# A trunk of attention and convolution on one core: four query tiles to a value product, and a quarter of the softmax combination on GpSimd

## The chip, the cores and the metric

One core of a Trainium2 chip (trn2). The metric is device time in microseconds of one launch; 2425.22 us is the median of three runs of the kernel before.

## What is computed

A float32 trunk of two layers over 1024 tokens of width 1024: differential attention with a convolutional feed-forward network behind it, then a gated short convolution with a second such network, then a norm. Only attention is touched by the change. For each of 8 heads:

```python
s = jnp.einsum('bqhcd,bkhcd->bhcqk', q_blk, k)          # c = 0, 1: two score maps
p = jax.nn.softmax(s, axis=-1)
a = p[:, :, 0] - lam * p[:, :, 1]
o = jnp.einsum('bhqk,bkhe->bqhe', a, v)                 # v is 128 wide
o = rms_norm(o, subln_g) * (1.0 - lambda_init)
```

## The kernel before

The program is written out by hand for each engine: every engine has its own list of instructions, which it works off in order, and semaphores tie them together. Matrix products keep float32 accuracy by splitting an operand into a rounded part (fp32r) and the rest, and summing three products. Activations lie with features on the 128 partitions.

The stages in order are: norm and projections to q, k, v, written to memory (till about 303 us); attention (303 to 645 us); output projection; feed-forward; convolution layer; second feed-forward. The output projection of the first two tiles (`dense_ahead`) already stands in the tail of attention.

**Attention** runs through 64 steps, 8 heads x 8 tiles of 128 queries. Each engine has a function `step(h, ii)` and `run_steps` calls them (steps of the middle heads in a hardware loop over pairs of heads). `i` counts the steps. PSUM has four slots of 1024 columns: slots 0 and 1 for the two score maps of a tile, one buffer each, slot 2 for transposes, slot 3 for the value product and, in its other half, the sum of squares.

What happens to a tile `i`, and in which step, is:

- TensorE, step i: `scores`, 4 products of 128x512 for each map (L656, L657). The first map waits for the first exponential of the tile before, the second map for the second one (`e_done`).
- VectorE, step i: `minimum` (L1281) over the 1024 columns of each map, the first and the second.
- ScalarE, step i: exponential of the first map (L962) into P0, with its row sum, and of the second map (L974) into P1. Between the two stands the rounding of the transposes of tile i-2 (L969).
- Step i+1: VectorE takes the reciprocal of a row sum (L1291) between its two minima; GpSimd makes the row's coefficient out of it in two small steps (L1549, L1552); VectorE combines the softmaxes, P1 = P1 * coef + P0 (L1300, called the combination below), 1024 columns. It is left unnormalised by the first row sum; that cancels in the norm behind it, if epsilon is scaled with the square of the row sum. GpSimd puts this square on a diagonal times epsilon (`dg`, L1558).
- Step i+2: TensorE transposes the combination, 8 blocks (L664); ScalarE rounds it (L969) into `Ah`; VectorE makes the rest (L1306) into `Al`.
- Once per pair of tiles: the value product (L679), 24 products of 256 columns, 12 in each of two steps; ScalarE copies it with a scale (L990) and squares it (L992); TensorE sums the squares and the epsilon diagonals over the partitions (L687, L690); ScalarE makes the factor (L983, L985); GpSimd multiplies (L1571); ScalarE rounds the result to Yh (L996) and GpSimd makes the rest Yl (L1565).

The order within a step is fixed: on TensorE scores, transposes, sum of squares, values; on ScalarE first exponential, rounding, second exponential, then the work of the pairs; on VectorE first minimum, reciprocal, second minimum, combination, rest; on GpSimd coefficient, square, diagonal, Yl, multiplication. SyncE loads K, Q and V of the next head, each once its buffer is free.

Of the kernel before, what the change touches and what calls it, by code (L numbers as in the profile page):

```python
# [80 lines left out]
def build(nc, x_in, positions, weights, ups, params_in, consts_in, lams_in, out):  # L81
    ctx = ExitStack()
    with ctx:
# [20 lines left out]
        coef = sb("coef", [P, 4])  # L104
        epsb = sb("epsb", [P, 1])
# [26 lines left out]
        W_more = at("W_more", [P, 2, 1024], AR + 70 * K, F32R)  # L132
        Wraw_more = at("Wraw_more", [P, 1024], AR + 70 * K + 4 * K)
# [52 lines left out]
        def q_set(h, parity):  # L186
            return 2 if is_first(h) else parity
# [42 lines left out]
        inv_done, co_done, a_done, t_done = sem("inverse_done"), sem("coef_done"), sem("a_done"), sem("t_done")  # L230
        ah_made, al_made = sem("ah_made"), sem("al_made")
        s0sq_done, dg_done = sem("s0sq_done"), sem("dg_done")
        pv_half = sem("pv_half")
# [132 lines left out]
        def lagged(q, first, tail):  # L366
            return (not first or q >= 0) and (not tail or q < QT)

        def on(q, first, tail):

            return q % 2 == 0 and lagged(q, first, tail)

        def run_steps(eng, step, last):
            for ii in range(QT):
                step(0, ii, first=True, parity=0)
            with eng.Fori(0, HEADS // 2 - 1) as pair:
                for a in range(2):
                    for ii in range(QT):
                        step(pair * 2 + (1 + a), ii, parity=1 - a)
            for ii in range(QT):  # L380
                step(HEADS - 1, ii, parity=1)
            for ii in range(QT, last + 1):
                step(HEADS - 1, ii, tail=True, parity=1)
# [22 lines left out]
        def _(sp):  # L406
# [84 lines left out]
            def load_head(h, parity, first=False):  # L491
# [8 lines left out]
                if not first:  # L500
                    sp.wait_ge(pv_done, 4 * (h - 1))
# [105 lines left out]
        def _(pe):  # L607
# [1120 lines left out]
```

## Time and profile before

| | |
|---|---|
| Median of 3 runs | 2425.22 us (2424.23 to 2425.43) |
| The profiled execution | 2422.12 us, span 2420.3 us |
| TensorE busy | 2350.3 us, 97% |
| VectorE busy | 1357.0 us, 56% |
| ScalarE busy | 949.7 us, 39% |
| GpSimd busy | 1050.0 us, 43% |
| Mean granted TensorE clock | 0.993 |

The shares are means over all stages. Rows name lines of the kernel before (L1300) and tiles as out<-in. PE is TensorE, PEld its weight loads, DVE VectorE, ACT ScalarE, POOL GpSimd. A matrix product's length in the trace has its fill in it; the distance from one start to the next is what it costs in a train of them.

### The profile page before, as it was taken

To read this page: it belongs to the slowest core of one execution; us is meant where nothing else is said; L and a number is where in the kernel's file an instruction comes from. 1 tells how busy PE (TensorE), PEld (TensorE's weight loads), DVE (VectorE), ACT (ScalarE), POOL (GpSimd) and SP (SyncE) were. 2 spreads that over 40 slices of the span, in tenths; PEclk is the share of its full clock that TensorE was granted. 3 is DMA by queue.
4 is the path that set the end of the run, shared out by engine and by line. 5 is a ranking of instruction groups with operands and counts; after the bars stand their busy time and mean duration, and the time that the engine had idled before them with its cause. 6 is when DMAs were issued, how large, how long until landed. Compare 5 with 4: busy or idle time off the path is not lost.

```text
span 2420.3 us, 28034 instructions
## 1 busy us (share of the span) xinstructions
PE 2350.3 (97%) x10948; PEld 1947.1 (80%) x10948; DVE 1357.0 (56%) x1240; ACT 949.7 (39%) x1149; POOL 1050.0 (43%) x725
## 2 busy tenths in 40 slices
PE   8899989999999999999999999999999999999997
PEld 6688778888877888888888888888878888888886
DVE  7566799999475555556422233344655555564223
ACT  5111278888444444444311321113454444442112
POOL 1112134444367677775122422213687666742221
PEclk9899999999999999999999999999999999999998
DMA  3453373432222222222522111112222222234222
GB/s 129 165 173 122 131 214 101 120 98 76 86 83 84 87 79 79 87 88 99 197 90 81 56 44 49 47 52 87 96 70 93 81 87 79 79 131 174 90 79 93
DMA packets 73799, 239.45 MB, mean 99 GB/s; under 512 B 8160, under 2 KB 8544, under 8 KB 73696
## 3 DMA queue, kind: packets, MB, share of 16 engines
q1 hardware_dynamic: 73696, 238.01, 29.9%
q8 instruction: 72, 1.18, 0.2%
q14 instruction: 31, 0.25, 0.0%
HBM read 177.16 MB, written 60.82 MB: 98 GB/s over the span
## 4 chain that ended last, share of the span: by engine, by line
PE 76%; issue 13%; ACT 4%; DVE 3%; POOL 3%; DMA 0%; POOLq 0%; DVEq 0%; ACTq 0%
PE PS L282 35%; PE PS L766 11%; PE PS L767 11%; PE PS L768 11%; PE PS L679 2%; DVE nb L1281 2%; POOL Wst L267 2%; PE PS L656 1%; PE PS L657 1%; PE PS L664 1%; ACT X L962 1%; ACT X L974 1%; ACT sq L974 1%; POOL X L1621 1%; PE PS L690 1%
## 5 line engine op out<-in xcount | busy, mean ns | idle before, releaser
L267 POOL TENSOR_TENSOR Wst<-Wraw,Wst 128x1024 fp32r<-128x1024 f32 (+1 forms) x111 | 263.0, 2371 | 877.5 <-ACT Wst L261 877.5
L766 PE MATMUL PS<-XB,U 128*128 128x512 f32 x1208 | 471.1, 390 | 6.9 <-POOL U L1615 6.8
L768 PE MATMUL PS<-XB,U 128*128 128x512 f32 x1224 | 476.7, 389 | 0.0
L282 PE MATMUL PS<-H,Wst 128*128 128x512 f32 x2070 | 470.1, 389 | 0.6 <-issue 0.3
L767 PE MATMUL PS<-XB,U 128*128 128x512 f32 x1208 | 470.4, 389 | 0.0
L282 PEld LDWEIGHTS PS<-H,Wst 128*128 128x128 f32 x2070 | 388.4, 188 | 81.9 <-issue 1.3
L282 PE MATMUL PS<-XGh,Wst 128*128 128x512 f32 x1536 | 420.3, 394 | 25.5 <-POOL Wst L267 13.0
L261 ACT ACTIVATE Wst<-Wraw 128x1024 fp32r<-128x1024 f32 (+1 forms) x111 | 113.9, 1028 | 652.3 <-DMA Wraw<-weights 652.2
L282 PEld LDWEIGHTS PS<-XGh,Wst 128*128 128x128 f32 x1536 | 290.1, 190 | 89.2 <-issue 24.6
L766 PEld LDWEIGHTS PS<-XB,U 128*128 128x128 f32 x1208 | 227.1, 188 | 55.9 <-POOL U L1615 7.6
L768 PEld LDWEIGHTS PS<-XB,U 128*128 128x128 f32 x1224 | 230.0, 188 | 48.0
L767 PEld LDWEIGHTS PS<-XB,U 128*128 128x128 f32 x1208 | 227.2, 188 | 46.8
L282 PE MATMUL PS<-XGl,Wst 128*128 128x512 f32 x768 | 239.0, 393 | 0.0
L1615 POOL TENSOR_TENSOR U<-U1f,U 128x2048 fp32r<-128x2048 f32 x44 | 203.8, 4631 | 6.0
L1077 ACT ACTIVATE PS<-rawg,par 128x1024 f32<-128x1024 f32 x44 | 53.2, 1210 | 385.9 <-DVE rawg L1400 385.9
L282 PEld LDWEIGHTS PS<-XGl,Wst 128*128 128x128 f32 x768 | 145.9, 190 | 30.8
L1281 DVE TENSOR_REDUCE nb<-PS 128x1 f32<-128x1024 f32 x128 | 154.1, 1210 | 15.9 <-PE PS L657 15.9
L1423 DVE TENSOR_TENSOR H<-Hf,H 128x1024 fp32r<-128x1024 f32 x44 | 71.2, 1619 | 142.0 <-ACT H L1086 141.8
L1615 POOL TENSOR_TENSOR U<-U2f,U 128x1536 fp32r<-128x1536 f32 x42 | 149.3, 3554 | 0.0
L1579 POOL TENSOR_TENSOR U1f<-U2f 128x512 f32<-128x512 f32 x44 | 57.9, 1316 | 208.0 <-DMA U2f<-ups 208.0
L282 PE MATMUL PS<-Yh,Wst 128*128 128x512 f32 x480 | 130.3, 390 | 2.7 <-POOL Wst L267 2.7
L1411 DVE SCALAR_TENSOR_TENSOR PS<-rawg,par,PS 128x1024 f32<-128x1024 f32 x88 | 113.4, 1289 | 28.6 <-ACT PS L1077 27.1
(191 smaller groups left out, 3311.2 us busy)
## 6 DMA issues: line engine op xcount, KB each, us to landing
Wraw<-weights SPq DMA_DIRECT2D x79, 512.0 KB, 3.5
U1f<-ups SPq DMA_DIRECT2D x44, 512.0 KB, 4.6
U2f<-ups SPq DMA_DIRECT2D x44, 512.0 KB, 3.8
h_scratch<-Tv SPq DMA_DIRECT2D x44, 512.0 KB, 5.4
Hf<-h_scratch SPq DMA_DIRECT2D x44, 512.0 KB, 4.7
Wraw<-weights SPq DMA_DIRECT2D x32, 448.0 KB, 3.2
x_scratch<-X SPq DMA_DIRECT2D x16, 512.0 KB, 3.1
X<-x_scratch SPq DMA_DIRECT2D x16, 512.0 KB, 7.1
```

The costliest lines, as they stand in the source:

```text
L261: act.activation(w[:, 0, 0:cols], raw[:, 0:cols], ACT.Copy).then_inc(w_hi, 1)
L267: pool.tensor_tensor(w[:, 1, 0:cols], raw[:, 0:cols], w[:, 0, 0:cols].bitcast(F32), ALU.subtract).then_inc(w_lo, 1)
L282: ins = pe.matmul(ps[:, h * HALF:(h + 1) * HALF], w, m[:, h * HALF:(h + 1) * HALF], start=begin, stop=last and w is wl)
L766: pe.matmul(ps, wh, bh, start=begin, stop=False, skip_group_check=True)
L767: pe.matmul(ps, wh, bl, start=False, stop=False, skip_group_check=True)
L768: ins = pe.matmul(ps, wl, bh, start=False, stop=kp == KP - 1, skip_group_check=True)
L1077: act.activation(conv_ps(kind), src[:, 1:S + 1], ACT.Identity, bias=ffn_col(l, p, kind, 3), scale=ffn_col(l, p, kind, 1)).then_inc(f["mid" ...
L1281: dve.tensor_reduce(nb[:, b:b + 1], slot(c), axis=AX_X, op=ALU.min).then_inc(nb_done, 1)
L1411: dve.scalar_tensor_tensor(out=T, in0=raw[:, off:off + S], scalar=ffn_col(l, p, kind, c), in1=T, op0=ALU.mult, op1=ALU.add).then_inc(f["ta ...
L1423: dve.tensor_tensor(Hs[t][:, 1, :], Hf[t][:, :], Hs[t][:, 0, :].bitcast(F32), ALU.subtract).then_inc(f["hl"], 1)
L1579: pool.tensor_tensor(U1f[s][:, 1, O_S1, :], U2f[s][:, 1, 1, :], U2f[s][:, 1, 2, :], ALU.add).then_inc(f["sums"], 1)
L1615: pool.tensor_tensor(u[s][:, 1, :, :], uf[s][:, 1, :, :], u[s][:, 0, :, :].bitcast(F32), ALU.subtract).then_inc(f["lo"], 1)
```

## The change

Four tiles of queries now go to one value product. `At` holds the rounded parts and the rests of two groups of four tiles; each group has one half of its own and one that both share. The value product is 24 products of 512 columns, of which 9, 12 and 3 stand in the steps ii-6, ii-7 and ii-8 of the group's first tile, the last 3 ahead of the transposes. ScalarE's and GpSimd's work on a result comes once in four steps and 512 columns wide, its order and its steps are new. The epsilon diagonals are added to the squares on GpSimd, and TensorE sums both with one instruction.

VectorE combines columns 0 to 767; GpSimd multiplies and then adds the last 256, each with an instruction of its own. Transposes and the next first exponential wait for both parts. There is no loop left: all 64 steps are written out. The third tile of the output projection (`W_more`) lies 2 KB further on. SyncE's waits on `pv_done` count groups of four. (`lagged` and `on` are as before, but with `q % 4`.)

```diff
-        Ah = [XGl[:, 2 * b:2 * b + 2, :].rearrange("p a (t n) -> p (a t) n", n=2 * P) for b in range(2)]
-        Al = [XGl[:, 4 + 2 * b:6 + 2 * b, :].rearrange("p a (t n) -> p (a t) n", n=2 * P) for b in range(2)]
-        osq, osb, z, ot = (sq[:, 0, t * 2 * P:(t + 1) * 2 * P] for t in range(4))
-        ot3 = sq[:, 0:1, 6 * P:8 * P]
-        dg = cu[:, 0:QT * P]
+            return 2 if h == 0 else parity
+        At = at("At", [P, 17, 2 * S], AR + 32 * K, F32R)
+        A_HI, A_LO = ((1, 16), (2, 16)), ((0, 4), (3, 4))
+        on_q = at("on_q", [P, 4, HALF], AR + 148 * K)
+        osq, osb, z, ot = (on_q[:, t, :] for t in range(4))
+        dg = at("dg", [P, HALF], ER + 16 * K)
+        def a_tile(where, q):
+            block = where[q // 4][q // 2 % 2]
+            return At[:, block, :].rearrange("p (t n) -> p t n", n=2 * P)[:, :, q % 2 * P:(q % 2 + 1) * P]
+        def a_group(where, g, t):
+            b0, b1 = where[g]
+            return At[:, b0:b1 + 1:b1 - b0, t * 2 * P:(t + 1) * 2 * P]
...
                 pe.wait_ge(a_done, i + 1)
+                pe.wait_ge(a_rest, i + 1)
                 wait(pe, al_made, i)
...
-            def values(h, u, quarter, part, parity):
-                b = quarter % 2
+            def values(h, u, g, part, parity):
                 if part == 0:
-                    pe.wait_ge(al_made, 2 * u + 2)
-                    wait(pe, o_sq, u)
-                if quarter == 0 and part == 0:
+                    pe.wait_ge(al_made, 4 * u + 4)
+                    wait(pe, o_copied, u)
+                if g == 0 and part == 0:
                     pe.wait_ge(v_in, 32 * (h + 1))
-                for t in range(4 * part, 4 * part + 4):
+                for t in (range(0, 3), range(3, 7), range(7, 8))[part]:
                     c = slice(t * P, (t + 1) * P)
-                    for w, m in ((0, Ah[b]), (0, Al[b]), (1, Ah[b])):
-                        first, last = t == 0 and w == 0 and m is Ah[b], t == KT - 1 and w == 1
-                        ins = pe.matmul(slot(3)[:, 0:2 * P], VV[parity][w][:, c], m[:, t, :], start=first, stop=last)
-                ins.then_inc((pv_half, pv_done)[part], 1)
-            def subln_sum(u, quarter):
-                pe.wait_ge(o_sq, u + 1)
-                pe.wait_ge(dg_done, 2 * u + 2)
+                    for w, m in ((0, A_HI), (0, A_LO), (1, A_HI)):
+                        first, last = t == 0 and w == 0 and m is A_HI, t == KT - 1 and w == 1
+                        ins = pe.matmul(slot(3)[:, 0:HALF], VV[parity][w][:, c], a_group(m, g, t),
+                                        start=first, stop=last)
+                if part == 2:
+                    ins.then_inc(pv_done, 1)
+            def subln_sum(u):
+                pe.wait_ge(sqd_done, u + 1)
                 wait(pe, ln_done, u)
-                pe.matmul(slot(3)[:, HALF:HALF + 2 * P], ones[:, :], osq, start=True, stop=False)
-                for t in range(2):
-                    b = 2 * quarter + t
-                    ins = pe.matmul(slot(3)[:, HALF + t * P:HALF + (t + 1) * P], ones[:, :],
-                                    dg[:, b * P:(b + 1) * P], start=False, stop=t == 1)
-                ins.then_inc(ss_done, 1)
+                pe.matmul(slot(3)[:, HALF:S], ones[:, :], osq, start=True, stop=True).then_inc(ss_done, 1)
...
+            def step(h, ii, tail=False):
+                i, parity = h * QT + ii, h % 2
...
+                if on(h, ii - 8, tail):
+                    values_of(8, 2)
+                if lagged(h, ii - 2, tail):
                     transposes(i - 2, (ii - 2) % QT)
-                if on(ii - 6, first, tail):
-                    subln_sum(h * 4 + (ii - 6) // 2, (ii - 6) // 2 % 4)
-                if on(ii - 4, first, tail):
-                    values(h, h * 4 + (ii - 4) // 2, (ii - 4) // 2 % 4, 0, parity if ii >= 4 else 1 - parity)
-                if on(ii - 5, first, tail):
-                    values(h, h * 4 + (ii - 5) // 2, (ii - 5) // 2 % 4, 1, parity if ii >= 5 else 1 - parity)
-                if tail:
-                    dense_ahead(*((0, (0, 1)), (0, (2, 3)), (0, (4, 5, 6)), (1, (0, 1, 2)), (1, (3, 4, 5, 6)))[ii - QT])
+                if on(h, ii - 10, tail):
+                    subln_sum(h * 2 + (ii - 10) // 4)
+                if on(h, ii - 6, tail):
+                    values_of(6, 0)
+                if on(h, ii - 7, tail):
+                    values_of(7, 1)
+                if tail and ii - QT in ahead:
+                    dense_ahead(*ahead[ii - QT])
...
+            def step(h, ii, tail=False):
                 i = h * QT + ii
                 if not tail:
                     act.wait_ge(nb_done, 2 * i + 1)
                     wait(act, a_done, i - 1)
+                    wait(act, a_rest, i - 1)
...
-                if lagged(ii - 2, first, tail):
+                if lagged(h, ii - 2, tail):
                     q = (ii - 2) % QT
                     act.wait_ge(t_done, i - 1)
-                    if q % 2 == 0:
-                        wait(act, pv_done, h * 4 + (ii - 2) // 2 - 1)
-                    act.activation(Ah[q // 2 % 2][:, :, q % 2 * P:(q % 2 + 1) * P],
-                                   slot(2).rearrange("p (t n) -> p t n", n=P), ACT.Copy).then_inc(ah_made, 1)
+                    if q % 4 == 0:
+                        wait(act, pv_done, h * 2 + (ii - 2) // 4 - 1)
+                    if q % 4 == 2:
+                        wait(act, pv_done, h * 2 + (ii - 2) // 4)
+                    act.activation(a_tile(A_HI, q), slot(2).rearrange("p (t n) -> p t n", n=P), ACT.Copy
+                                   ).then_inc(ah_made, 1)
...
+                if on(h, ii - 10, tail):
...
                     act.wait_ge(ss_done, u + 1)
...
+                    wait(act, o_scaled, u)
+                    act.activation(z, slot(3)[:, HALF:S], ACT.Ln, scale=1.0 / VD).then_inc(ln_done, 1)
...
+                if on(h, ii - 8, tail):
+                    u = h * 2 + (ii - 8) // 4
                     act.wait_ge(pv_done, u + 1)
+                    wait(act, ss_done, u)
+                    act.activation(osq, slot(3)[:, 0:HALF], ACT.Square).then_inc(o_sq, 1)
                     wait(act, o_scaled, u)
-                    act.activation(osb, slot(3)[:, 0:2 * P], ACT.Copy, scale=lam[:, 5:6]).then_inc(o_copied, 1)
-                    wait(act, ss_done, u)
-                    act.activation(osq, slot(3)[:, 0:2 * P], ACT.Square).then_inc(o_sq, 1)
-                if on(ii - 8, first, tail):
-                    u, uq = h * 4 + (ii - 8) // 2, (ii - 8) // 2
+                    act.activation(osb, slot(3)[:, 0:HALF], ACT.Copy, scale=lam[:, 5:6]).then_inc(o_copied, 1)
...
+                if on(h, ii - 12, tail):
+                    u = h * 2 + (ii - 12) // 4
                     act.wait_ge(o_scaled, u + 1)
-                    act.activation(Yh[:, bass.ds(h + uq // 4, 1), uq % 4 * 2 * P:(uq % 4 + 1) * 2 * P], ot3, ACT.Copy
+                    act.activation(Yh[:, u // 2, u % 2 * HALF:(u % 2 + 1) * HALF], ot, ACT.Copy
                                    ).then_inc(yh_made, 1)
...
-                    dve.scalar_tensor_tensor(out=P1[q % 4], in0=P1[q % 4], scalar=coef[:, 3:4],
-                                             in1=P0[q % 2], op0=ALU.mult, op1=ALU.add).then_inc(a_done, 1)
-                if lagged(ii - 2, first, tail):
+                    dve.scalar_tensor_tensor(out=P1[q % 4][:, main_cols], in0=P1[q % 4][:, main_cols],
+                                             scalar=coef[:, 3:4], in1=P0[q % 2][:, main_cols], op0=ALU.mult,
+                                             op1=ALU.add).then_inc(a_done, 1)
...
+                    dve.tensor_tensor(a_tile(A_LO, q), slot(2).rearrange("p (t n) -> p t n", n=P),
+                                      a_tile(A_HI, q).bitcast(F32), ALU.subtract).then_inc(al_made, 1)
...
+                    wait(pool, a_rest, i - 1)
                     pool.tensor_tensor(coef[:, 3:4], coef[:, 1:2], rsum[:, 0, q:q + 1], ALU.mult).then_inc(co_done, 1)
-                    wait(pool, dg_done, i - 1)
-                    pool.tensor_tensor(coef[:, 2:3], rsum[:, 0, q:q + 1], rsum[:, 0, q:q + 1], ALU.mult
+                    pool.wait_ge(co_done, 2 * i)
+                    rest = P1[q % 4][:, rest_cols]
+                    pool.tensor_tensor(rest, rest, coef[:, 3:4].to_broadcast([P, S // 4]), ALU.mult
+                                       ).then_inc(a_scaled, 1)
+                    pool.wait_ge(a_scaled, i)
+                    pool.tensor_tensor(rest, rest, P0[q % 2][:, rest_cols], ALU.add).then_inc(a_rest, 1)
...
-                    wait(pool, ss_done, h * 4 + (ii - 9) // 2 + 2)
-                    pool.tensor_tensor(dg[:, q * P:(q + 1) * P], con[:, C_EPSI:C_EPSI + P],
-                                       coef[:, 2:3].to_broadcast([P, P]), ALU.mult).then_inc(dg_done, 1)
-                if on(ii - 9, first, tail):
-                    u, uq = h * 4 + (ii - 9) // 2, (ii - 9) // 2
-                    dst = bass.ds(h + uq // 4, 1), slice(uq % 4 * 2 * P, (uq % 4 + 1) * 2 * P)
+                if on(h, ii - 13, tail):
+                    u = h * 2 + (ii - 13) // 4
+                    cols = slice(u % 2 * HALF, (u % 2 + 1) * HALF)
                     pool.wait_ge(yh_made, u + 1)
-                    pool.tensor_tensor(Yl[:, dst[0], dst[1]], ot3, Yh[:, dst[0], dst[1]].bitcast(F32), ALU.subtract
+                    pool.tensor_tensor(Yl[:, u // 2, cols], ot, Yh[:, u // 2, cols].bitcast(F32), ALU.subtract
                                        ).then_inc(yl_made, 1)
-                if on(ii - 7, first, tail):
-                    u = h * 4 + (ii - 7) // 2
+                if lagged(h, ii - 6, tail):
+                    q = (ii - 6) % QT
+                    pool.wait_ge(s0sq_done, i - 5)
+                    if q % 4 == 0:
+                        wait(pool, sqd_done, h * 2 + (ii - 6) // 4)
+                    pool.tensor_tensor(dg[:, q % 4 * P:(q % 4 + 1) * P], con[:, C_EPSI:C_EPSI + P],
+                                       s0sq[:, q:q + 1].to_broadcast([P, P]), ALU.mult).then_inc(dg_done, 1)
+                if on(h, ii - 9, tail):
+                    u = h * 2 + (ii - 9) // 4
+                    pool.wait_ge(dg_done, 4 * u + 4)
+                    pool.wait_ge(o_sq, u + 1)
+                    pool.tensor_tensor(osq, osq, dg[:, :], ALU.add).then_inc(sqd_done, 1)
+                if on(h, ii - 11, tail):
+                    u = h * 2 + (ii - 11) // 4
                     pool.wait_ge(z_done, u + 1)
+                    pool.wait_ge(o_copied, u + 1)
                     wait(pool, yl_made, u)
                     pool.tensor_tensor(ot, osb, z, ALU.mult).then_inc(o_scaled, 1)
```

The instructions of GpSimd, one step and the wide work behind it, in a head inside the loop. Before:

```order
L1549 TENSOR_TENSOR coef<-coef,lam 128x1
L1550 ISA
L1552 TENSOR_TENSOR coef<-coef,rsum 128x1
L1554 TENSOR_TENSOR coef<-rsum 128x1
L78 REGISTER_ALU
L1558 TENSOR_TENSOR cu<-con,coef 128x128
L1565 ISA
L1565 TENSOR_TENSOR Yl<-sq,Yh 128x256
L1571 TENSOR_TENSOR sq<-sq 128x256
```

And now (L1573 and L1576 are product and addition of the last 256 columns, L1585 is Yl, L1598 the addition of the diagonals, `on_q` holds the squares and the results):

```order
L1566 TENSOR_TENSOR coef<-coef,lam 128x1
L1570 TENSOR_TENSOR coef<-coef,rsum 128x1
L1573 TENSOR_TENSOR X<-X,coef 128x256
L1576 TENSOR_TENSOR X<-X 128x256
L1578 TENSOR_TENSOR s0sq<-rsum 128x1
L1585 TENSOR_TENSOR Yl<-on_q,Yh 128x512
L1592 TENSOR_TENSOR dg<-con,s0sq 128x128
L1598 TENSOR_TENSOR on_q<-on_q,dg 128x512
```

Product and addition are new in every step; the addition of the diagonals, for the sum of squares, stands last in this one.

TensorE, from the transposes of a step with a sum of squares on. Before:

```order
L657 MATMUL PS<-Yl 128x512
L664 MATMUL PS<-con,X 128x128 x8
L687 MATMUL PS<-sq,ones 128x256
L690 MATMUL PS<-cu,ones 128x128 x2
L679 MATMUL PS<-XGl,Xr 128x256 x12
```

And now, with the scores and transposes of the following step (L665 and L666 are the scores, L674 the transposes, L697 the sum, L688 the values):

```order
L697 MATMUL PS<-on_q,ones 128x512
L688 MATMUL PS<-At,Xr 128x512 x9
L665 MATMUL PS<-XGh 128x512
L666 MATMUL PS<-XGh 128x512
L665 MATMUL PS<-XGh 128x512
L666 MATMUL PS<-XGh 128x512
L665 MATMUL PS<-XGh 128x512
L666 MATMUL PS<-XGh 128x512
L665 MATMUL PS<-XGh 128x512
L666 MATMUL PS<-XGh 128x512
L674 MATMUL PS<-con,X 128x128 x8
L688 MATMUL PS<-At,Xr 128x512 x12
```

The sum is one instruction on 512 columns, 9 value products follow it, and 12 follow the next transposes.

## Rows read from the trace of the kernel before

**Rows 1.** Windows: length, busy per engine (instructions), TensorE clock, DMA share, GB/s
```profile
362.28:599.35 237.07, 227.23 (x1489) 198.67 (x1490) 226.16 (x242) 195.61 (x360) 103.17 (x241) 1.00 0.36 93
316.00:325.00 9.00, 6.28 (x32) 4.52 (x32) 9.00 (x11) 6.14 (x11) 1.56 (x8) 1.00 1.04 243
```
**Rows 2.** Timeline, two steps: TensorE. Start, length, engine, line, out<-in, [idle before]
```profile
460.91 0.50 PE L656 MATMUL PS<-Yh,Xr 128*128 128x512 f32 x1 [0.42 <-ACT sq L974]
...
461.95 1.04 PE L664 MATMUL PS<-con,R 128*128 128x128 f32 x8
...
462.83 0.60 PE L687 MATMUL PS<-sq,ones 128*128 128x256 f32 x2
...
463.26 0.61 PE L690 MATMUL PS<-cu,ones 128*128 128x128 f32 x4
...
463.62 1.68 PE L679 MATMUL PS<-XGl,XGh 128*128 128x256 f32 x12
...
465.14 0.40 PE L656 MATMUL PS<-Yh,Xr 128*128 128x512 f32 x1
...
466.99 1.04 PE L664 MATMUL PS<-con,sq 128*128 128x128 f32 x8
...
467.78 1.68 PE L679 MATMUL PS<-XGl,XGh 128*128 128x256 f32 x12
```
**Rows 3.** Timeline, the same steps: VectorE, ScalarE and the next scores
```profile
466.27 1.23 DVE L1281 TENSOR_REDUCE nb<-PS 128x1 f32<-128x1024 f32 x1 [0.38 <-PE PS L657]
...
467.48 1.21 DVE L1281 TENSOR_REDUCE nb<-PS 128x1 f32<-128x1024 f32 x1
467.53 1.11 ACT L962 ACTIVATE X<-PS,nb 128x1024 f32<-128x1024 f32 x1 [0.90 <-DVE nb L1281]
...
468.60 1.28 DVE L1300 SCALAR_TENSOR_TENSOR X<-X,coef 128x1024 f32<-128x1024 f32 x1
468.64 1.02 ACT L969 ACTIVATE XGl<-PS 128x1024 fp32r<-128x1024 f32 x1
...
469.54 1.12 ACT L974 ACTIVATE X<-PS,nb 128x1024 f32<-128x1024 f32 x1
...
469.81 1.21 DVE L1306 TENSOR_TENSOR XGl<-PS,XGl 128x1024 fp32r<-128x1024 f32 x1
...
470.80 0.50 PE L656 MATMUL PS<-Yh,Xr 128*128 128x512 f32 x1 [0.40 <-ACT X L974]
...
470.95 1.21 DVE L1281 TENSOR_REDUCE nb<-PS 128x1 f32<-128x1024 f32 x1
```
**Rows 4.** Timeline, the same steps: GpSimd, the coefficient
```profile
467.64 0.19 POOL L1549 TENSOR_TENSOR coef<-coef,lam 128x1 f32<-128x1 f32 x1 [3.97 <-DVE coef L1291]
...
467.91 0.19 POOL L1552 TENSOR_TENSOR coef<-coef,rsum 128x1 f32<-128x1 f32 x1
```
**Rows 5.** Timeline: GpSimd beside VectorE's combination, two places
```profile
463.27 0.40 POOL L1558 TENSOR_TENSOR cu<-con,coef 128x128 f32<-128x128 f32 x1 [0.17 <-POOL coef L1554]
463.38 1.37 DVE L1300 SCALAR_TENSOR_TENSOR sq<-sq,coef,X 128x1024 f32<-128x1024 f32 x1
...
616.77 1.28 DVE L1300 SCALAR_TENSOR_TENSOR R<-R,coef,X 128x1024 f32<-128x1024 f32 x1
...
616.86 1.78 POOL L1565 TENSOR_TENSOR Yl<-sq,Yh 128x256 fp32r<-128x256 f32 x1
```
**Rows 6.** Lines of GpSimd with 256 and 512 columns: ns min/median/max
```profile
L1571 POOL TENSOR_TENSOR sq<-sq x32: 726/736/1789, 340.3 to 645.8; 128x256 f32<-128x256 f32 x32
...
L1579 POOL TENSOR_TENSOR U1f<-U2f x44: 1287/1296/1747, 689.3 to 2131.3; 128x512 f32<-128x512 f32 x44
```
**Rows 7.** A line of ScalarE with 512 columns out of PSUM
```profile
L1005 ACT ACTIVATE sP<-PS x132: 573/580/602, 727.6 to 2154.1; 128x512 f32<-128x512 f32 x132
```
**Rows 8.** Timeline, VectorE: first minimum of step 12 and of step 60
```profile
362.28 1.21 DVE L1281 TENSOR_REDUCE nb<-PS 128x1 f32<-128x1024 f32 x1
...
599.35 1.21 DVE L1281 TENSOR_REDUCE nb<-PS 128x1 f32<-128x1024 f32 x1
```

More of the change, by code:

```diff
@@ L104, in build @@
         coef = sb("coef", [P, 4])
+        s0sq = sb("s0sq", [P, QT])
         epsb = sb("epsb", [P, 1])
@@ L361, in conv_col, with lagged, on, run_steps @@
             return par[:, bass.ds(ft * 3 + (C_CONV + c), 1)]
[L366 to L381, printed above, removed]
+        def lagged(h, q, tail):
+            return h * QT + q >= 0 and (not tail or q < QT)
+        def on(h, q, tail):
+            return q % 4 == 0 and lagged(h, q, tail)
+        main_cols, rest_cols = slice(0, 3 * S // 4), slice(3 * S // 4, S)
+        def run_steps(step, last):
+            for h in range(HEADS):
+                for ii in range(QT):
+                    step(h, ii)
             for ii in range(QT, last + 1):
-                step(HEADS - 1, ii, tail=True, parity=1)
+                step(HEADS - 1, ii, tail=True)
         def bank(p, role):
@@ L500, in load_head @@
                 if not first:
-                    sp.wait_ge(pv_done, 4 * (h - 1))
+                    sp.wait_ge(pv_done, 2 * (h - 1))
                 sp.wait_ge(v_in, 32 * h)
@@ L705, in dense_ahead, with values_of @@
                     ins.then_inc(tile_done, 1)
[L707 to L708 removed]
+            def step(h, ii, tail=False):
+                i, parity = h * QT + ii, h % 2
                 if not tail:
                     scores(h, i, ii, parity)
[L711 removed]
+                if i == 0:
                     v_transpose(HEADS - 1)
[L713 removed]
+                if i == 2:
                     pe.wait_ge(rot_read, 2 * HEADS)
                     pe.wait_ge(vl_made, HEADS)
[L716 to L725 removed]
+                def values_of(lag, part):
+                    q = ii - lag
+                    values(h + q // QT, h * 2 + q // 4, q // 4 % 2, part, (h + q // QT) % 2)
+                if on(h, ii - 8, tail):
+                    values_of(8, 2)
+                if lagged(h, ii - 2, tail):
+                    transposes(i - 2, (ii - 2) % QT)
+                if on(h, ii - 10, tail):
[6 more added lines that the diff above has]
+                    dense_ahead(*ahead[ii - QT])
             pe.wait_ge(v_out, HEADS)
             pe.wait_ge(rot_read, 2 * HEADS - 1)
[L729 removed]
+            run_steps(step, 14)
             def dense(d, base):
@@ L955, in _ @@
             act.preload_act_table_set("natural_log_exp_and_others")
-            def step(h, ii, first=False, tail=False, parity=0):
+            def step(h, ii, tail=False):
                 i = h * QT + ii
@@ L1281, in minimum, with step @@
                 dve.tensor_reduce(nb[:, b:b + 1], slot(c), axis=AX_X, op=ALU.min).then_inc(nb_done, 1)
-            def step(h, ii, first=False, tail=False, parity=0):
+            def step(h, ii, tail=False):
                 i = h * QT + ii
@@ L1287, in step @@
                     minimum(i, ii, 0)
-                if lagged(ii - 1, first, tail):
+                if lagged(h, ii - 1, tail):
                     dve.wait_ge(e_done, 2 * i)
@@ L1541, in _, with step @@
             pool.wait_ge(lam_done, 2)
-            def step(h, ii, first=False, tail=False, parity=0):
+            def step(h, ii, tail=False):
                 i = h * QT + ii
-                if lagged(ii - 1, first, tail):
+                if lagged(h, ii - 1, tail):
                     q = (ii - 1) % QT
@@ L1571, in step @@
                     pool.tensor_tensor(ot, osb, z, ALU.mult).then_inc(o_scaled, 1)
-            run_steps(pool, step, 15)
+            run_steps(step, 17)
             def up_sums(l, p, part):
```

45 lines of the change are left out of this document (17 added, 28 removed).

## The prediction

> **What bounds the kernel now.** Only the attention stage is touched, so I first cut the trace into windows. In a steady stretch of 48 steps (a step is one tile of 128 queries of one head) TensorE is busy 227.2 of 237.1 us and VectorE 226.2, while ScalarE and GpSimd have room [rows 1]. Two engines near full do not say which wait ends last, so I read the timeline of two steps. It repeats every two steps, because the values and the sum of squares come in pairs of tiles. The closed chain in it is: the first minimum of the odd step (466.27) releases the first exponential (467.53), behind it on ScalarE stands the evacuation of the transposes (468.64), then the second exponential (469.54), whose end releases the second scores of the next step (470.80) [rows 3]. One such start earlier (460.91) TensorE runs without a gap through transposes, sum, values and the next first scores to the next minimum at 466.27 [rows 2, 3]. The sum: 1.26 + 1.11 + 0.90 + 1.26 us outside TensorE and 5.36 us (460.91 to 466.27) on it give 9.89 us for two steps. The 48 steps take 599.35 - 362.28 = 237.07 us, 9.88 for two [rows 8]: this chain is the pace. VectorE alone would allow 4.68 (466.27 to 470.95 without a wait [rows 3]).
>
> **The change, part by part.** I number steps modulo 4, r0 to r3, and set the start of the first minimum of r0 to 0.
>
> *TensorE.* 24 products of 256 columns per pair stand 0.127 us apart (467.78 to 469.30; 465.14 - 463.62 = 1.52 for 12 [rows 2]). The 24 products of 512 per four tiles should stand as the scores do, four in 466.07 - 465.14 = 0.93, so 0.232 each; the scores' second half starts so. Four tiles: 48 x 0.127 = 6.1 us become 24 x 0.232 = 5.6. The sum of squares has one instruction in two passes; 256 columns take 463.26 - 462.83 = 0.43 us, 512 will take 0.86, and the four of 128 go (463.62 - 463.26 = 0.36): per four tiles 1.58 becomes 0.86 [rows 2]. So TensorE saves 1.2 us per four steps. But what it has left is less even: r2 gets the sum and 9 products (2.95 us), r3 12 products (2.78), r0 3 (0.70), r1 none.
>
> *VectorE.* The combination of the softmaxes shrinks from 1.28 to 768/1024 of its columns. With a fixed part (1.28 for 1024; minima and subtractions unchanged) I put it at 1.01. GpSimd starts its product at the same coefficient. The coefficient's two steps start at +1.37 and +1.64 [rows 3, 4]; one more such distance puts the 256 column product at +1.91, and it takes 0.74 [rows 6], till 2.65. VectorE's combination would start at +2.32 (468.60 less 466.27 [rows 3]). Both read SBUF alone. What that does is seen twice: a GpSimd subtraction of 256 columns issued 0.09 us behind a combination took 1.78 and ended 0.59 after it (0.74 is its usual time); a combination issued while GpSimd was at work ended 463.38 + 1.37 = 464.75, 1.08 after GpSimd's end [rows 5, 6]. So one waits for the other, and here VectorE does: the combination ends at 2.65 + 1.08 - 0.27 = 3.46, not 3.33. The step of VectorE becomes about 4.55 (it was 4.68): of 0.27 saved, half stays.
> The Trainium skill (SBUF — State Buffer, "SBUF: two separate sides") calls the pair of ports these two share an exclusive lock that the first holds for its whole instruction, the other blocked. The rows of a late GpSimd instruction agree; for a late VectorE one they show only 0.1 us lost of the 0.29 of overlap. By the rule the combination would run its full 1.01 behind 2.65, each step in the chain would be 0.2 longer, and the total some 5 us above mine.
>
> *ScalarE.* Per four tiles ten instructions of 256 become five of 512 (0.58 for 512 columns out of PSUM [rows 7]), but three of them (square, scaled copy, Yh) now stand together in r0, about 1.65 us.
>
> *GpSimd.* New are product and addition in every step; the three wide instructions (Yl, addition of the epsilon diagonal, product with the factor) are 512 wide, 1.30 each against 0.74 [rows 6]. Two of them stand in r1, one behind the other, and the sum of squares of r2 on TensorE waits for the second. The dynamic Yl write and the loop branches go; I cost that at nothing, since GpSimd was idle 3.97 us before the coefficient [rows 4].
>
> *DMA.* The same loads; V waits for values done one or two steps later, with a head's time to spare: nothing.
>
> **The sum.** r0: minimum 0, exponentials 1.26 and 3.27, the three wide ones till 6.0; the minimum of r1 at 4.55 would allow 5.81, so ScalarE goes on at 6.0, its second exponential starts at 8.0, and the second scores of r2 at 9.27. Transposes from 10.31, the sum of squares could start at 11.15. GpSimd in r1: product till 4.55 + 2.65; the addition waits for VectorE's combination (till 4.55 + 3.46) and ends 0.59 later, at 8.6; square of the row sum, Yl 1.30, diagonal 0.40, addition 1.30 with the small gaps: 12.1. So TensorE waits 0.95 us there. Then 0.86 + 2.09 (9 products) + 1.86 (scores) + 0.79 (transposes) + 2.78 (12 products) + 1.13 (first scores till the minimum starts, 466.27 - 465.14) = 9.5: the next r0 at 21.6 us. Before, four steps took 237.07 / 12 = 19.76. That is 1.85 more, 12 times = 22 us; the block before (no Yl yet) and the last three steps add about 2.5, the tail, with the same products in another order, nothing (within 1 us). I take +25. The profiled execution, 2422.12 us around a span of 2420.3, becomes 2447; it lies 3.1 below the median of 2425.22, so the median becomes **2450**.
>
> TensorE will be busy some 17 of 21.6 us. At 6.28 of 9.00 us busy the granted clock was still 1.00 (2.4 GHz) [rows 1], so I cost no clock.
>
> **Bounds.** Unknown are GpSimd's durations beside VectorE. Below: its work in r1 ends before 11.15, and the four-step chain alone holds, 20.65. Above: each of the two wide ones takes 1.75 and the product loses the race for the port in every step (0.6 more): 23.1, +18 us on mine.
>
> **Rivals.**
> A, the forecast: GpSimd's r1 ends last, 2450 (2442 to 2458). 0.48.
> B, the chain of TensorE's ten-microsecond train and ScalarE's two steps alone, GpSimd in time: 12 x 0.9 + 2 = +13, 2438. For it: GpSimd is only 0.95 late, by estimated gaps. 0.22.
> C, GpSimd worse than its rows, by the upper bound: 2458 to 2468. 0.15.
> D, faster: the uneven train doesn't matter, because VectorE falls behind it and catches up, so the rates decide. VectorE then sets 4.55 against 4.94 a step, 59 steps x -0.39 = -23 us, 2402. It decides if the chain from the second scores of r2 round to themselves is below 19.76 without GpSimd; I get 20.65, and two score slots of one buffer each leave nothing to run ahead on. For it: both near-full engines have less work. The Trainium skill (Perfetto Trace Analysis, "Optimizing Scalar/DVE Operations") says that work moved from VectorE to GpSimd might not help, as they share a read port; no more than that part of D hangs on it. 0.10.
> E, the two effects cancel within 5 us: 2425. 0.05.
> That the change doesn't do what it says: the order of the instructions shows that it does.
>
> **The numbers.** About 0.2% (5 us) can be told from no change. Faster is D, 0.10; same E, 0.05; slower A, B and C, 0.85. For 8 in 10: A, B and most of C, 2431 to 2466.
>
> **What would show it.** In the changed profile: steps of about 5.4 us in the mean, in blocks of four of unequal length (from r0: about 4.55, 4.8, 7, 5.3); TensorE idle before the 512 column sum of squares, released by GpSimd, near 1 us, 15 times; GpSimd's addition near 1.5 us with its wait; combinations of 1.1 to 1.2 us; VectorE idle before first minima of r3 and r0. Wrong is A if TensorE doesn't wait there, and A and B both if the blocks of four are equal steps or below 19.8 us.

## The result and the profile after

| | before | change |
|---|---|---|
| median of four runs | 2424.72 us | 2440.82 us (2437.85 to 2442.04) |
| the profiled execution | 2422.12 us, span 2420.3 | 2440.23 us, span 2438.4 |

The ratio is 1.0064, 95% interval 1.0049 to 1.0080: 16 us slower. The forecast was 2450 (25 slower), with a range of 2431 to 2466.

The page of the change, busy time per engine:

```profile
span 2438.4 us, 26394 instructions
...
PE 2342.0 (96%) x10404; PEld 1908.3 (78%) x10404; DVE 1348.5 (55%) x1240; ACT 938.9 (39%) x1069; POOL 1154.9 (47%) x837
...
DVE  7567688888465555556522233434655555564223
ACT  5121267777555444444211321113444334442112
POOL 1112167777667776676122422122677766742221
```

GpSimd has 105 us more than before, VectorE only 8.5 less and TensorE 8 less. I read the stage where the work changed. The window from step 12 to step 60, as in [rows 1]:

```profile
361.76:617.80 256.04, 222.54 (x1081) 169.66 (x1080) 222.93 (x240) 186.85 (x300) 180.85 (x325) 1.00 0.34 87
```

The 48 steps take 256.04 us, not 237.07 [rows 8]: a block of four steps takes 21.34 against 19.76, +19.0 us in all. TensorE and VectorE are both at 87%, where they stood at 96 and 95%. The twelve steps before add 1.9 us, the last three 0.8, the tail (first minimum of step 63 to the third output tile) gives back 1.1. From there on both kernels take 1768 us. Attention began 2.4 us earlier than before; in the runs below this start wanders from 301.0 to 305.7 us with the code ahead of it unchanged. So I compare blocks of steps, not totals, wherever a microsecond matters.

The timeline of one block, only the rows of the chain and of the shared port (L1298 first minimum, L976 first exponential, L1317 combination, L1573 and L1576 GpSimd's product and addition, L1585 Yl, L1598 addition of the diagonals, L697 sum of squares, L688 values, L665 scores, L674 transposes, L985 rounding, L1323 rest):

```profile
457.53 1.27 POOL L1598 TENSOR_TENSOR on_q<-on_q,dg 128x512 f32<-128x512 f32 x1
...
458.86 1.12 PE L697 MATMUL PS<-on_q,ones 128*128 128x512 f32 x2 [0.37 <-POOL on_q L1598]
...
459.25 1.47 DVE L1317 SCALAR_TENSOR_TENSOR X<-X,coef 128x768 f32<-128x768 f32 x1 [0.38 <-POOL coef L1570]
459.30 0.61 POOL L1573 TENSOR_TENSOR X<-X,coef 128x256 f32<-128x256 f32 x1
...
459.42 2.64 PE L688 MATMUL PS<-At,XGh 128*128 128x512 f32 x9
...
461.89 0.39 PE L665 MATMUL PS<-XGh 128*128 128x512 f32 x1
...
464.50 2.99 PE L688 MATMUL PS<-At,XGh 128*128 128x512 f32 x12
...
467.33 0.39 PE L665 MATMUL PS<-Yh,Xr 128*128 128x512 f32 x1
...
468.44 1.23 DVE L1298 TENSOR_REDUCE nb<-PS 128x1 f32<-128x1024 f32 x1 [0.80 <-PE PS L666]
...
469.70 1.12 ACT L976 ACTIVATE X<-PS,nb 128x1024 f32<-128x1024 f32 x1 [2.22 <-DVE nb L1298]
...
469.83 1.03 PE L674 MATMUL PS<-con,R 128*128 128x128 f32 x8
...
470.35 0.61 POOL L1573 TENSOR_TENSOR sq<-sq,coef 128x256 f32<-128x256 f32 x1
...
470.77 1.01 DVE L1317 SCALAR_TENSOR_TENSOR sq<-sq,coef,X 128x768 f32<-128x768 f32 x1
...
470.90 1.03 ACT L985 ACTIVATE At<-PS 128x1024 fp32r<-128x1024 f32 x1
...
471.05 1.33 POOL L1576 TENSOR_TENSOR sq<-sq,X 128x256 f32<-128x256 f32 x1
...
471.96 1.22 DVE L1323 TENSOR_TENSOR At<-PS,At 128x1024 fp32r<-128x1024 f32 x1 [0.18 <-ACT At L985]
...
473.11 1.21 DVE L1298 TENSOR_REDUCE nb<-PS 128x1 f32<-128x1024 f32 x1
...
474.48 1.13 ACT L976 ACTIVATE X<-PS,nb 128x1024 f32<-128x1024 f32 x1
...
476.66 1.22 DVE L1323 TENSOR_TENSOR At<-PS,At 128x1024 fp32r<-128x1024 f32 x1 [0.20 <-ACT At L985]
...
477.15 1.27 POOL L1585 TENSOR_TENSOR Yl<-on_q,Yh 128x512 fp32r<-128x512 f32 x1
...
478.38 0.40 POOL L1592 TENSOR_TENSOR dg<-con,s0sq 128x128 f32<-128x128 f32 x1
...
478.80 1.03 PE L674 MATMUL PS<-con,X 128*128 128x128 f32 x8
...
478.87 1.27 POOL L1598 TENSOR_TENSOR on_q<-on_q,dg 128x512 f32<-128x512 f32 x1
...
480.19 0.70 PE L697 MATMUL PS<-on_q,ones 128*128 128x512 f32 x1 [0.36 <-POOL on_q L1598]
```

The block from 458.86 to 480.19 is the forecast chain nearly row for row. From the sum of squares TensorE runs without a gap through 9 values, scores, transposes, 12 values to the scores at 467.33, whose first minimum starts at 468.44: 9.58 us from the start of the sum, 9.5 were forecast. r0's first minimum to r1's (473.11) takes 4.67. GpSimd's addition of the diagonals ends at 480.14 and the sum starts at 480.19, after 0.36 us without a matrix product. The loss is larger than this idle time, since a row's length has its fill in it: from the start of the transposes to the start of the sum are 1.39 us, and 0.88 before the change [rows 2], so 0.51 us. Waits in the window, in total and times:

```profile
DVE nb L1298 <- PE PS L666: 24.0, 25, 1.2
...
PEld PS L697 <- POOL on_q L1598: 7.1, 12, 0.6
```

The sum waits for GpSimd once in every block, 12 times for 0.6 us (the wait of its weight load), and 13 times in the whole stage, where I had forecast 15, and VectorE's minimum waits for the scores 25 times, about two a block: behind the trains of r2 and r3, as forecast.

### The profile page after: what moved, and what is told of

It reads as the page before. It is cut to its first block, busy times and chain, and to the rows that moved or that the text cites. A ratio compares the mean times of both kernels' runs of the same rounds, so it can differ in the third digit from the quotient of the medians.

```text
span 2438.4 us, 26394 instructions
## 1 busy us (share of the span) xinstructions
PE 2342.0 (96%) x10404; PEld 1908.3 (78%) x10404; DVE 1348.5 (55%) x1240; ACT 938.9 (39%) x1069; POOL 1154.9 (47%) x837
## 4 chain that ended last, share of the span: by engine, by line
PE 70%; issue 16%; POOL 12%; DVE 1%; ACT 1%; DMA 0%; POOLq 0%; SPq 0%; DVEq 0%; ACTq 0%
PE PS L293 35%; PE PS L779 11%; PE PS L780 11%; PE PS L781 11%; POOL X L1576 2%; POOL Wst L278 2%; POOL sq L1576 1%; POOL dg L1592 1%; POOL R L1576 1%; POOL X L1573 1%; POOL on_q L1604 1%; POOL Yl L1585 1%; POOL X L1654 1%; POOL coef L1570 1%; POOL coef L1566 0%
## 5 line engine op out<-in xcount | busy, mean ns | idle before, releaser
L1298 DVE TENSOR_REDUCE nb<-PS 128x1 f32<-128x1024 f32 x128 | 154.9, 1216 | 31.2 <-PE PS L666 31.2
```

The lines of the kernel that those rows point to most:

```text
L1298: dve.tensor_reduce(nb[:, b:b + 1], slot(c), axis=AX_X, op=ALU.min).then_inc(nb_done, 1)
```

## The experiments

All are variants of the change (e2: of the kernel before). "Block" is four steps between step 12 and step 60, as above.

| run | what | median us | ratio to before (95%) | block us |
|---|---|---|---|---|
| before | | 2424 to 2427 | 1 | 19.76 |
| change | | 2440.82 | 1.0064 (1.0049 to 1.0080) | 21.34 |
| e1 | groups, no split | 2437.23 | 1.0046 (1.0029 to 1.0062) | 20.87 |
| e2 | pairs, split | 2446.66 | 1.0085 (1.0069 to 1.0102) | 21.33 |
| e3 | change, Yl a step later | 2436.45 | 1.0042 (1.0027 to 1.0057) | 20.72 |
| e4 | change, values 6, 9, 9 | 2445.80 | 1.0084 (1.0067 to 1.0101) | 21.44 |
| e7 | e1, wide GpSimd work waits | 2440.09 | 1.0056 (1.0039 to 1.0073) | 21.03 |
| e5 | values 6, 6, 6, 6, no split, waits | 2416.19 | 0.9960 (0.9945 to 0.9974) | 19.18 |
| e8 | e5 without the waits | 2441.16 | 1.0065 (1.0048 to 1.0082) | 21.05 |
| e6 | values 6, 6, 6, 6, split | 2412.09 | 0.9943 (0.9927 to 0.9960) | 19.16 |
| e9 | e6 with 7, 3, 7, 7 | 2407.91 | 0.9928 (0.9910 to 0.9945) | 18.46 |
| e10 | e5 with 7, 3, 7, 7 | 2406.76 | 0.9919 (0.9901 to 0.9938) | 18.63 |

**e1, the groups alone.**

```diff
-        main_cols, rest_cols = slice(0, 3 * S // 4), slice(3 * S // 4, S)
+        main_cols = slice(0, S)
-                pe.wait_ge(a_rest, i + 1)
-                    pool.tensor_tensor(rest, rest, coef[:, 3:4].to_broadcast([P, S // 4]), ALU.mult
-                                       ).then_inc(a_scaled, 1)
...
-                    pool.tensor_tensor(rest, rest, P0[q % 2][:, rest_cols], ALU.add).then_inc(a_rest, 1)
```

> The change with its four-tile groups, but VectorE combines all 1024 columns again and GpSimd's product and addition are gone. Theory 1 (the uneven train of value products sets a four-step chain, GpSimd's lateness only adds the 0.36 us that TensorE waits ahead of the sum of squares): blocks of four steps of 20.97 to 21.1 us, no wait of the sum for GpSimd, 13 x 0.36 = 4.7 us less than the change, 2436. Rival (the cost is GpSimd's share of the combination): it goes back to the kernel before or below it, blocks of at most 19.8 us, at most 2425.

2437.23 us: the grouping alone is 11 us slower than the kernel before, against 16 of the change, and the rival falls. The block is 20.87, a little below the expected 20.97. But it is not the expected block inside. Its steps are 4.65, 5.33, 5.18, 5.71 from r0 (means), and VectorE's combination (L1314) takes 1.95 and 2.32 us in two of four steps. GpSimd's Yl (L1575) and its multiplication (L1594) now come before it:

```profile
535.46 1.27 POOL L1575 TENSOR_TENSOR Yl<-on_q,Yh 128x512 fp32r<-128x512 f32 x1
...
535.87 1.95 DVE L1314 SCALAR_TENSOR_TENSOR X<-X,coef 128x1024 f32<-128x1024 f32 x1
...
546.34 1.29 POOL L1594 TENSOR_TENSOR on_q<-on_q 128x512 f32<-128x512 f32 x1
546.39 2.33 DVE L1314 SCALAR_TENSOR_TENSOR R<-R,coef,X 128x1024 f32<-128x1024 f32 x1
```

The combination was issued 0.05 us behind the multiplication, took 2.33 in place of 1.27 us, and ended 1.09 after GpSimd's end (547.63). So the split had a hidden use: product and addition stand ahead of the wide instructions and keep them behind VectorE's combination (e6 and e8 below bear this out).

**e2, the split alone**, on the kernel before with its pairs.

```diff
+                    pool.wait_ge(co_done, 2 * i)
+                    rest = P1[q % 4][:, 3 * S // 4:S]
+                    pool.tensor_tensor(rest, rest, coef[:, 3:4].to_broadcast([P, S // 4]), ALU.mult
+                                       ).then_inc(a_scaled, 1)
+                    pool.wait_ge(a_scaled, i)
+                    pool.tensor_tensor(rest, rest, P0[q % 2][:, 3 * S // 4:S], ALU.add).then_inc(a_rest, 1)
```

> The kernel before with its pairs, and only the last 256 columns moved to GpSimd. Theory 1 (GpSimd's queue is what a split loads): Yl and the multiplication stand behind product and addition, so the multiplication ends 1.3 us later than before, the copy that waits for it on ScalarE too, and the sum of squares behind that by 0.9; two steps take 10.8 instead of 9.88 us, 32 times 0.9 = 29, some 2450. Rival (the split gives VectorE 0.13 to 0.27 us a step and TensorE's chain hides the rest): 2417 to 2425.

2446.66 us, block 21.33, so 10.67 for two steps (10.8 expected). GpSimd's queue is what a split loads. The timeline shows Yl (L1576), the multiplication (L1582), ScalarE's copy behind it after 1.76 us idle (0.72 before), its square and the sum of squares:

```profile
502.91 0.73 POOL L1576 TENSOR_TENSOR Yl<-sq,Yh 128x256 f32 x1
...
503.78 0.73 POOL L1582 TENSOR_TENSOR sq<-sq 128x256 f32<-128x256 f32 x1
...
504.61 0.47 ACT L993 ACTIVATE sq<-PS,lam 128x256 f32<-128x256 f32 x1 [1.76 <-POOL sq L1582]
...
504.98 0.38 ACT L995 ACTIVATE sq<-PS 128x256 f32<-128x256 f32 x1
...
505.40 0.70 PE L689 MATMUL PS<-sq,ones 128*128 128x256 f32 x2 [0.43 <-ACT sq L995]
```

From the start of the transposes to the sum are 1.46 us here, and 0.88 before. Alone, each of the two parts slows the kernel, and together they cost no more than the split alone. That this is because in groups of four GpSimd's wide work comes half as often is my reading; no run shows it.

**e3, Yl one step later.** `on(h, ii - 13, tail)` of Yl becomes `on(h, ii - 14, tail)`.

> The change with Yl one step later (r2 in place of r1), so that the addition that the sum of squares waits for comes 1.3 us earlier on GpSimd. Theory 1: TensorE no longer waits ahead of the sum, block 20.97 us, 4.7 us less than the change, 2436. If GpSimd's r1 were a larger part than its visible wait (because it also delays VectorE's coefficient in r2 by 0.38 us), it falls by more, to 2430. Rival (GpSimd not on the chain): 2441, no change.

2436.45 us; no wait of the sum for GpSimd is left in the list of waits, the block falls by 0.61, all of it in r2, between the two figures expected:

```profile
518.12 1.04 PE L674 MATMUL PS<-con,X 128*128 128x128 f32 x8
...
519.00 1.02 PE L697 MATMUL PS<-on_q,ones 128*128 128x512 f32 x2
```

Transposes to sum are 0.88 us again, which gives 0.51. The other 0.10 lies between the start of the sum and the next first minimum, 4.15 us in the change and 4.05 here. So the wait is worth 0.61 by itself, what its weight load showed, and not the 0.36 of idle time. VectorE's late combination in r2 (1.47 us at 459.25 above) costs nothing, as the next first minimum waits for TensorE anyway.

**e4, values 6, 9, 9** in place of 9, 12, 3.

```diff
-                for t in (range(0, 3), range(3, 7), range(7, 8))[part]:
+                for t in (range(0, 2), range(2, 5), range(5, 8))[part]:
```

> The change with the 24 value products split 6, 9, 9 over the steps r2, r3, r0 in place of 9, 12, 3. Theory 1 (the chain also runs through the transposes of r0, that stand behind that step's value products): TensorE's train from r2 to r0 gets 1.4 us shorter, but the transposes of r0 start 1.4 us later, and with them the rounding, VectorE's rest and the first minimum of r1; block 21.2 against 21.33, 2439 to 2441. Rival (only the length of the train up to the scores of r0 counts): block 19.95, 17 to 18 us less, 2423.

2445.80 us, block 21.44, 0.24 and 5 us above what I expected: no gain from a train 1.4 us shorter (the rival said 19.95), since the transposes of r0 stand behind 9 products. Transposes, ScalarE's rounding, VectorE's rest and the next first minimum:

```profile
536.71 1.03 PE L674 MATMUL PS<-con,R 128*128 128x128 f32 x8
...
537.78 1.02 ACT L985 ACTIVATE At<-PS 128x1024 fp32r<-128x1024 f32 x1 [1.48 <-PE PS L674]
...
538.83 1.22 DVE L1323 TENSOR_TENSOR At<-PS,At 128x1024 fp32r<-128x1024 f32 x1 [1.66 <-ACT At L985]
...
539.98 1.21 DVE L1298 TENSOR_REDUCE nb<-PS 128x1 f32<-128x1024 f32 x1
```

VectorE waits 1.66 us for the rounding and r0 is 6.14 us long. So what counts is where a product stands in the two chains through r0, not the length of one train. The total is 5.0 us above the change, and only 1.2 of it lies in the blocks from 12 to 60. The last three steps add 0.8, the stretch from step 63 to the third output tile 0.4, the code behind that, which is the same, 2.1; attention starts 1.5 later, and its first twelve steps are 0.9 shorter.

**e7, e1 with waits.** Ahead of each of GpSimd's wide instructions: `wait(pool, a_done, i)`.

> The groups alone (as e1_group_only, no split), and GpSimd's three wide instructions wait until VectorE's combination of the same step is done. In e1_group_only two of them got ahead of the combination, which then took 1.95 and 2.32 us and VectorE's steps 5.33 and 5.72. Theory: both go back to 1.28, the steps r1 and r3 get 0.7 and 0.3 us shorter where VectorE is on the chain; the four-step chain of TensorE's train remains, so the block is 20.7 to 20.9 against 20.87: at most 2 us less, 2435 to 2437. Rival (these collisions, not the train, make e1_group_only slow): block 19.8 or less, at most 2424.

2440.09 us, block 21.03: the combinations are at 1.28 again, but nothing is won, which refutes the rival and lies 0.1 above my range. Yl now starts 1.7 us later, and behind it the addition of the diagonals ends at 541.16, so that the sum of squares waits for it again:

```profile
538.13 1.28 POOL L1577 TENSOR_TENSOR Yl<-on_q,Yh 128x512 fp32r<-128x512 f32 x1 [1.73 <-DVE X L1314]
...
539.89 1.27 POOL L1592 TENSOR_TENSOR on_q<-on_q,dg 128x512 f32<-128x512 f32 x1
```

The wait is smaller than in the change: transposes to sum are 1.10 us, and the whole comes to 0.3 a block. Without it the block would be 20.7, as in e3. So 20.7 is what the placing 9, 12, 3, 0 gives with neither a collision nor a wait for GpSimd, with the split (e3) and without it (e7).

**e5, an even train.** Products with the rests first, 6 per step, behind the transposes; block 5 of `At` doubles the second half of the rounded parts; the sum of squares at ii-11; Yl, multiplication, Yh and additions at ii-15, ii-12, ii-13 and ii-10; `W_more` loaded when all values are done; no split; GpSimd's wide instructions wait as in e7.

```diff
+                jobs = [(0, A_LO, t) for t in range(KT)] + [(w, A_HI, t) for w in range(2) for t in range(KT)]
+                for j in range(6 * part, 6 * part + 6):
...
+                for part in range(4):
+                    if on(h, ii - 6 - part, tail):
+                        values_of(6 + part, part)
```

> Groups of four, no split, but the 24 value products stand 6, 6, 6, 6 in four steps, behind the transposes. For that one more 8 KB block doubles the second half of the rounded parts, the products with the rests come first, the third output tile's weights are loaded after attention, and the sum of squares stands one step later, the work behind it two. GpSimd's wide instructions wait for the combination. Theory (the uneven train is what costs): two-step chain 4.58 + 1.03 + 0.79 + 1.36 + 1.11 = 8.9 us, with the sum 9.8, so 18.7 for four steps, VectorE 4 x 4.68 = 18.7; block 18.7 to 18.9, 13 x 0.95 = 12 us less than the kernel before, 2412 to 2415. Rival (groups of four cost whatever the distribution, through lags or ScalarE's 512 column work): at or above the kernel before.

2416.19 us, faster than before by 0.40% (0.26 to 0.55). The block is 19.18, 0.3 above the expected range: three steps are 4.65, and the one behind the sum and 6 products is 5.20. Against e7, which has the same groups, wide instructions and waits, the placing in the steps changed: 24 us less, 1.85 a block, and the sign with it. The new placing is more than an even train. No product stands ahead of the transposes any more (3 did, in r0), and GpSimd's Yl and addition, both in r1 before, have steps of their own; of the 1.85 this last is worth at most the 0.3 that the sum waited in e7. So where the work stands is the cause, and the larger groups are not. How much is the evenness and how much the place behind the transposes no run separates; that evenness counts by itself is seen in e9 and e10.

**e8, e5 without the waits.**

> As e5_even_wait, without the wait of GpSimd's wide instructions for the combination. Theory (whichever takes the shared port first holds it for the whole instruction): where a wide instruction starts before the combination, this takes about 2.3 in place of 1.28 us; up to 1 us in two or three of four steps of VectorE, which is on the chain here; block 20.5 to 21.7, 2432 to 2450. Rival (no lasting effect, as VectorE catches up): as e5_even_wait.

2441.16 us, block 21.05: 25 us for three waits. The combination takes 2.32, 1.97 and 1.97 us in three of four steps. With e7 this says that each of the two faults alone holds the block at 21.0, the uneven train in e7 and the collisions here; only without both does it fall. Two of the collisions (L1575 Yl, L1594 the multiplication, L1312 the combination):

```profile
502.76 1.30 POOL L1575 TENSOR_TENSOR Yl<-on_q,Yh 128x512 fp32r<-128x512 f32 x1
...
503.18 1.97 DVE L1312 SCALAR_TENSOR_TENSOR R<-R,coef,X 128x1024 f32<-128x1024 f32 x1
...
508.47 1.30 POOL L1594 TENSOR_TENSOR on_q<-on_q 128x512 f32<-128x512 f32 x1
508.52 2.32 DVE L1312 SCALAR_TENSOR_TENSOR sq<-sq,coef,X 128x1024 f32<-128x1024 f32 x1
```

**e6, the even train with the split**, no waits.

> The even distribution with the split of the change (VectorE 768 columns, GpSimd 256), no added wait: product and addition keep GpSimd's wide instructions behind the combination. Theory: VectorE's step falls to 4.55 to 4.66, the two-step chain stays, GpSimd has at most one wide instruction a step; block 18.5 to 18.8, 2410 to 2414. Rival (GpSimd, near 4.2 us of work in a step with its waits for VectorE, comes late with the coefficient): block above 19.2, above 2418.

2412.09 us, block 19.16 (18.5 to 18.8 expected). Against the change itself, which has the split and no waits too, this placing is worth 29 us; against e3, where the sum does not wait for GpSimd either, 24 us or 1.56 a block. The combination takes 1.01 or 1.02 us in all four steps: GpSimd's addition keeps the wide work behind it, without a semaphore. The step with the sum is 5.27 here (5.20 in e5), so TensorE's chain holds the block; e9 bears this out.

**e9 and e10, 7, 3, 7, 7 products**, with the split and without.

```diff
-                for j in range(6 * part, 6 * part + 6):
+                for j in (range(0, 7), range(7, 10), range(10, 17), range(17, 24))[part]:
```

> e6_even_split with the 24 products split 7, 3, 7, 7, so that the step with the sum of squares (0.94 us, as long as four products) has 3. Theory (the two-step chain holds in the step pairs with the sum: there 6 products and the sum make a step of 5.27 us beside steps of 4.6): that step falls by 3 x 0.23 = 0.7, the others rise by at most 0.23 where VectorE does not cover it; block 18.5 to 18.7 against 19.16, 6 to 8 us less than e6_even_split, 2404 to 2407. Rival (VectorE or GpSimd holds the block already): within 2 us of e6_even_split.

> e5_even_wait with 7, 3, 7, 7. Without the split VectorE's four steps are 4 x 4.68 = 18.7 at the least. Theory: block 18.7 to 18.8, 5 us less than e5_even_wait, 2410 to 2412, so that the split is worth some 3 to 5 us once TensorE's chain is even. Rival: no difference between this and e9_balanced_split, the split is worth nothing anywhere.

2407.91 and 2406.76 us: both intervals lie wholly below the kernel before, by 0.72% and 0.81%, and they overlap. I had expected 2404 to 2407 and 2410 to 2412, 3 to 5 us for the split; in the medians the rival holds, no difference. The blocks are 18.46 and 18.63, at or just below the expected ranges (18.5 to 18.7 and 18.7 to 18.8), so in the one profiled execution of each the split is worth 0.17 a block, some 2 us of the stage; in e6 against e5 it was worth nothing. Of the 0.7 a block that e9 has less than e6, all is in the step of the sum, as forecast. In e10 all four steps are 4.65 us, VectorE's instructions end to end; GpSimd's wide one (L1577) starts behind the combination, beside VectorE's work out of PSUM, and ends before the next coefficient:

```profile
522.48 1.22 DVE L1293 TENSOR_REDUCE nb<-PS 128x1 f32<-128x1024 f32 x1
...
524.81 1.28 DVE L1312 SCALAR_TENSOR_TENSOR R<-R,coef,X 128x1024 f32<-128x1024 f32 x1
...
526.00 1.22 DVE L1320 TENSOR_TENSOR At<-PS,At 128x1024 fp32r<-128x1024 f32 x1
...
526.16 1.29 POOL L1577 TENSOR_TENSOR Yl<-on_q,Yh 128x512 fp32r<-128x512 f32 x1 [1.71 <-DVE R L1312]
...
527.13 1.22 DVE L1293 TENSOR_REDUCE nb<-PS 128x1 f32<-128x1024 f32 x1
```

## Why the prediction was right, and where it was off

- *The pace of the kernel before, and what takes its place*: right. A closed chain from row to row gave 9.89 for two steps, and its counterpart for four gave 21.6 for the change; 21.34 was measured. Without GpSimd it gave 20.65, and e3 measured 20.72. The steps from r0 were forecast as 4.55, 4.8, 7, 5.3 and are 4.67, 4.69, 6.55, 5.43. e6 against e3 and e5 against e7 show the placing as the cause: it took each from slower than before to faster.
- *GpSimd's addition comes last before the sum of squares*: right in place, too large in size. Counted from the first minimum of r0 the addition ends at 11.70 us and the sum starts at 11.75, 12.1 were forecast: the product takes 0.61, not 0.74, and Yl 1.27, not 1.30, and the gaps were estimates. Without GpSimd the sum could have started at 11.24; I had 11.15, where rows 2 give 11.19. So the wait is 0.51, not 0.95, and with what follows it 0.61 a block (e3).
- *The number*: the case A and its rival B differ by this one wait. At half its size the median, 2440.82, falls between A's 2450 and B's 2438, nearer to B, and just below the 2442 to 2458 that I gave to A. The mechanism is A's, since TensorE does wait there; the price is not. That the range holds it owes something to its width.
- *VectorE's step of 4.55*: 4.67 and 4.69 measured in r0 and r1, for another reason than those I weighed. In three of four steps GpSimd's short product was through the port early enough, and the combination took 1.01. But in r0 and r1 VectorE's rest waited 0.2 us for ScalarE's rounding. In r3 the rest starts 3.42 us behind the first minimum, in r0 3.52 and in r1 3.55. In r0 the transposes, behind scores and values, end 0.1 us too late for the rounding. In r1 it is the first exponential that starts 1.37 behind its minimum in place of 1.26 (474.48 above), behind ScalarE's three wide instructions. My sum gave VectorE's step only its own instructions and left out that the rounding follows both the transposes and the first exponential.
- *The lock of the shared port*: in e1 and e8 the combination came second and ran 1.07 to 1.09 us of its 1.27 after GpSimd's end, as my row had it (1.08 after). By the Trainium skill's rule (SBUF — State Buffer, "SBUF: two separate sides"), the later one blocked for the whole of the first, it would be the full 1.27; the runs show 0.2 less. The 0.2 us a step that I set between the two did not arise, as in three of four steps nothing was blocked and in r2 VectorE is not on the chain.
- *Costed at nothing*: DMA and clock, right (granted clock 1.00 in the window). TensorE was busy 18.5 us of a block, not some 17; nothing hung on it. The tail I put within 1 us gave 1.1.
- *Total*: 22 + 2.5 were forecast, 19.0 + 2.7 - 1.1 measured in the stage, less 2.4 of the wandering start; 16 in the medians.
- *Rival D, faster* through the rates, fell: TensorE and VectorE both went down to 87% busy. Nor did any single bound decide: e2 and e1 are each slower than before, for different waits.

Still open: how much of the gain of e5 and e6 is the evenness and how much the place behind the transposes, and why the stretches outside attention, with the same code, differ by some microseconds from run to run.

## What to carry to other kernels

In a pipeline whose buffers hold one step, the sum of an engine's work says little: walk the chain over the whole period in which the pattern repeats, and put the same load into each step of it before putting it into fewer instructions. Here wider matrix products cost 11 to 15 us when they stood 9, 12, 3, 0 (e1, e7) and gained 17 to 20 at 7, 3, 7, 7, the step of the sum relieved (e9, e10).

Wide GpSimd work that reads SBUF is best tied to the end of VectorE's instruction with two SBUF inputs; here it was free beside work out of PSUM, and cost 0.7 to 1.0 us each time when it started just ahead of that instruction (e8).

## What was unexpected of the hardware

- By the recorded starts the first to be issued is not always the one that gets the port. In the change's block above VectorE's combination starts at 459.25 and GpSimd's product at 459.30; the product takes its usual 0.61, and the combination 1.47 in place of 1.01, ending 0.81 after the product. It is so in all 12 blocks, though 0.05 us is little to rest an order of starts on. My estimate is that a combination needs the port only some 0.2 us after its recorded start: a product that ended 0.19 us after it, at 470.96, cost it nothing, one that ended 0.29 after it cost 0.1 [rows 5], and a blocked combination runs 0.2 less than its length behind GpSimd's end.
- A product of a [128x256] tile with a broadcast column takes 0.61 us on GpSimd, an operation on two such tiles 0.74 [rows 6]; the change's addition took 1.33 with the wait for VectorE's combination.
